# A four-branch decoder trunk: the HGRN forget-gate sigmoids taken from ACT's Sigmoid

## The chip, the core and the metric

The kernel runs on one core of one Trainium2 chip. The metric is device time in microseconds (us), the median of three executions: 3426.57 us, between 3426.15 and 3428.24. Engines are named as in the profile: PE is TensorE (matmuls; PEld is its weight loading), DVE is VectorE, ACT is ScalarE, POOL is GpSimd, SP is SyncE. A name with a q (DVEq, ACTq) is that engine's sequencer. PEclk is the clock granted to TensorE, where 1.00 is 2.4 GHz and 0.50 is 1.2 GHz.

## What is computed

Two layers over 256 tokens at width 2048. In each layer a normalised input h goes through one wide projection, and four token mixers run on slices of it (gated DeltaNet, HGRN2, a diagonal S5, retention), each 1024 wide. They are gated, projected, merged and added to the stream. All is float32. The change touches the HGRN branch only:

```python
def hgrn2_branch(q, f_logit, i_in, g, lb, norm_w):
    q = jax.nn.silu(q)
    log_f = jnp.log(lb + (1.0 - lb) * jax.nn.sigmoid(f_logit))
    k = (1.0 - lb) * jax.nn.sigmoid(-f_logit)
    o = hgrn2_chunked(to_chunks(q), to_chunks(k), to_chunks(i_in), to_chunks(log_f))
    return head_rmsnorm_gate(from_chunks(o), norm_w, g)
```

So both sigmoid(f) and sigmoid(-f) of the forget logit f are needed, for every channel and token.

## The kernel before

**Layout.** Channels lie on the 128 partitions and tokens along the free dimension. A "unit" is 128 channels of every branch (one head each); a layer has 8 units, run as a hardware loop, so there are 16 unit passes. After a layer's units come the GLU of S5, the merge (16 output tiles) and the output projection.

**A unit.** Its frame is the projection: 14 blocks of 128 columns, each in two halves of 8 weight tiles, so 28 calls `project(0)` to `project(27)` on PE. Each call is 24 matmuls, as every product is made from three passes over high and low parts (`w_hi`, `w_lo`, `h_hi`, `h_lo`). Blocks alternate between two PSUM banks, PJ0 and PJ1. The first blocks are HF (the forget logit, halves 0 and 1), GK (2 and 3), GQ (4 and 5), SU (6 and 7) and HQ (8 and 9).

**The weights.** They pass through a ring of four slots. SP's queue loads a half into `raw_w`; ACT copies it to `w_hi` (line 516); DVE subtracts to give `w_lo` (line 896) and so also frees the raw slot. `ahead(i)` on ACT and on DVE makes the copy and the subtraction for the half that `project(i + 4)` uses.

**The order** is written out by hand on each engine. Each engine runs its list strictly in order, and semaphores join the lists. On PE: project(0), project(1), `g_decay_t` (bank GB), project(2), `g_decay_s` (GB), project(3), project(4), `s_turn`, project(5), (6), (7), `g_norms` (GB: sums of squares of the DeltaNet keys and queries, eight matmuls with one moving column), `g_gram_k` (GA), project(8), `s_bu(0)`, `g_gram_q`, project(9), `g_first` (GA), project(10) and so on; from there on a step of the DeltaNet inversion (GA) and a step of HGRN's pairs (`h_pairs`, bank HA) stand between the projections.

On ACT, the start of a unit is: `ahead(0)`, `decays_t` (three exponentials, line 559), the two exponentials of the forget logit (lines 624 and 625), `ahead(1)`, `decays_s` (two exponentials, line 565), two `Sin` for S5 (lines 631, 632), `ahead(2)`, staging of GK (571, 572), `ahead(3)`, a square (637), the copy of `bc_T` (640), `silu_conv(0)` (581, 584), `ahead(4)`, staging of GQ, `ahead(5)`, `silu_conv(1)` (581, 584). The last of these is what `g_norms` waits for. Activation tables are loaded by ACT_TABLE_LOAD instructions that the compiler puts in; they carry the line of the instruction behind them.

On DVE the exponentials become sigmoids: wait for `hsig_staged`, add 1 to both (line 1099), a reciprocal of `hsig[:, 0]` (line 1101), and much later, after `s5_turn(0)` and `ahead(9)`, a reciprocal of `hsig[:, 1]` (line 1148). Then `s5_add(0)` (1033, 1034), and `hf` and `hk` are made from them (1152, 1153). PE's `h_pairs(0)` waits for these. `pj_read`, raised by ACT's second exponential, frees bank PJ0 for `project(4)`.

HGRN's scan is then 8 stages: PE's `h_pairs(s)` gives a bank, DVE's `h_scores(s)` (1058 to 1072) takes it over and rescales the operands for the next stage; its DRAIN on line 1072 frees the bank.

Of the kernel before, what the change touches and what calls it, by code (L numbers as in the profile page):

```python
# [120 lines left out]
def trunk_kernel(nc, A, out):  # L121
    f32, f32r, u8, i32 = mybir.dt.float32, mybir.dt.float32r, mybir.dt.uint8, mybir.dt.int32
    ALU, ACT = mybir.AluOpType, mybir.ActivationFunctionType
    ds = bass.ds
    ctx = ExitStack()
    with ctx:
# [6 lines left out]
        def sem(name):  # L133
            return ctx.enter_context(nc.semaphore(name))
# [67 lines left out]
        def in_work(*shape):  # L202
            n0 = work_at[0]
            work_at[0] += math.prod(shape)
            v = work[:, n0:work_at[0]]
            return v if len(shape) == 1 else v.rearrange("p (a n) -> p a n", a=shape[0])
# [23 lines left out]
        hsig = in_work(2, SEQ)  # L230
# [68 lines left out]
        pj_read = sem("pj_read")  # L299
# [12 lines left out]
        hsig_staged, hsig_used = sem("hsig_staged"), sem("hsig_used")  # L312
# [172 lines left out]
        def _(act):  # L485
            A_ = nc.scalar.activation
# [24 lines left out]
            def split_hi(i, s0, r0):  # L511


                act.wait_ge(split_used, s0 + (i + 1))
                act.wait_ge(raw_full[i % RING], r0 * 16 + 16 * (i // RING + 1))
                A_(w_hi[i % RING][:, :, :], raw_w[i % RING][:, :, :], ACT.Copy).then_inc(hi_ready, 1)  # L516

            with act.Fori(0, DEPTH) as l:
# [21 lines left out]
                with act.Fori(0, UNITS) as u:  # L540
                    n = act.snap(l * UNITS + u)
                    n1 = act.snap(n + 1)
# [4 lines left out]
                    def projected(b):  # L547

                        act.wait_ge(split_used, s0 + (2 * b + 2 + RING))
                        return PJ[b % 2][:, 0:SEQ]  # L550

                    def ahead(i):

                        split_hi(i + RING, s0, r0)

                    def decays_t():
                        act.wait_ge(gb_w, gb0 + 1)
                        for a, c in enumerate((C_NGC0, C_SUF0, C_NGC1)):
                            last = A_(dec_t[:, a, :], GB[:, a * P:(a + 1) * P], ACT.Exp, bias=gcols[:, c:c + 1])
                        last.then_inc(gb_r, 1)  # L560

                    def decays_s():
                        act.wait_ge(gb_w, gb0 + 2)
                        for a, c in enumerate((C_GC0, C_GC1)):
                            last = A_(dec_s[:, a, :], GB[:, a * P:(a + 1) * P], ACT.Exp, bias=gcols[:, c:c + 1])
                        last.then_inc(gb_r, 1)
# [52 lines left out]
                    act.wait_ge(gdn_qkv_used, n1)  # L619
                    decays_t()  # L620

                    act.wait_ge(hsig_used, n1)
                    src = projected(B_HF)
                    A_(hsig[:, 0, :], src, ACT.Exp, scale=-1.0)
                    A_(hsig[:, 1, :], src, ACT.Exp).then_inc(pj_read, 1)
                    act.drain().then_inc(hsig_staged, 1)
                    ahead(1)
                    decays_s()

                    act.wait_ge(phase_ready, l + n1)  # L630
                    A_(s5_sin, s5_p, ACT.Sin, scale=SIN_TURN)
# [151 lines left out]
        def _(dve):  # L783
            TS, TT, STT = nc.vector.tensor_scalar, nc.vector.tensor_tensor, nc.vector.scalar_tensor_tensor
# [108 lines left out]
            def split_lo(i, s0):  # L893

                dve.wait_ge(hi_ready, s0 + (i + 1))
                TT(w_lo[i % RING][:, :, :], raw_w[i % RING][:, :, :], w_hi[i % RING][:, :, :].bitcast(f32),  # L896
                   ALU.subtract).then_inc(raw_used[i % RING], 1)
# [5 lines left out]
            with dve.Fori(0, DEPTH) as l:  # L903
# [77 lines left out]
                with dve.Fori(0, UNITS) as u:  # L981
                    n = dve.snap(l * UNITS + u)
                    n1 = dve.snap(n + 1)
# [18 lines left out]
                    def ahead(i):  # L1002

                        split_lo(i + RING, s0)
# [25 lines left out]
                    def s5_add(half):  # L1030

                        j = slice(2 * half, 2 * half + 2)
                        TT(s5_re[:, j], s5_p[:, 0:2], s5_q[:, 0:2], ALU.add)
                        TT(s5_im[:, j], s5_p[:, 2:4], s5_q[:, 2:4], ALU.subtract)
                        dve.drain()  # L1035
# [59 lines left out]
                    ahead(0)  # L1095
                    ahead(1)

                    dve.wait_ge(hsig_staged, n1)
                    TS(hsig[:, :, :], hsig[:, :, :], 1.0, None, ALU.add)
                    dve.drain()  # L1100
                    nc.vector.reciprocal(hsig[:, 0, :], hsig[:, 0, :])
                    ahead(2)
                    conv_taps(0)
                    ahead(3)
# [40 lines left out]
                    dve.wait_ge(sincos_ready, n1)  # L1145
                    s5_turn(0)
                    ahead(9)
                    nc.vector.reciprocal(hsig[:, 1, :], hsig[:, 1, :])
                    s5_add(0)
                    dve.wait_ge(hgrn_used, n1)  # L1150
                    lb0, lb1 = (lb[:, ds(u, 1), c:c + 1].rearrange("p a b -> p (a b)") for c in range(2))
                    TS(hf[:, :], hsig[:, 0, :], lb1, lb0, ALU.mult, ALU.add)
# [134 lines left out]
                with dve.Fori(0, MT) as t:  # L1287
# [3 lines left out]
                    for pair in range(2):  # L1291
                        for i in range(6 * pair, 6 * pair + 4):
                            split_lo(i + RING, s0)
                        for m in (2 * pair, 2 * pair + 1):
# [5 lines left out]
                            src = (SA, SB)[m % 2][:, 0:SEQ]  # L1300
# [492 lines left out]
```

## Time and profile before

| What | Value |
|---|---|
| Three executions | 3426.15, 3426.57, 3428.24 us |
| Profiled execution, first to last instruction (span) | 3423.5 us; the profile gives no other time of it |
| PE busy | 3199.7 us (93%), 25656 matmuls |
| DVE busy | 2193.0 us (64%) |
| ACT busy | 1446.7 us (42%) |
| POOL busy | 286.3 us (8%) |
| Mean granted TensorE clock | 0.975 |
| One unit pass | about 117 us, 16 of them |

The page of the profile has the busy time of each engine, the span in 40 slices, the DMA queues, the chain of work that ended last, and the costliest groups of instructions. The trace can also be asked for the waits, the chain in order of time, the timeline of one engine, and the busy time and clock of a chosen stretch. PE's matmuls overlap in the timeline: each 128x256 one is shown as 0.28 us, but they start 0.12 us apart at the full clock.

### The profile page before, as it was taken

What the parts mean: (1) busy time and instruction counts of PE and PEld (TensorE: products, weight loads), DVE (VectorE), ACT (ScalarE), POOL (GpSimd) and SP (SyncE); (2) the same over time, 40 slices, a digit from 0 to 9 for tenths busy, and PEclk for the clock granted to TensorE, in tenths of its full rate; (3) what the DMA queues carried; (4) which work ended last, traced back from release to release, by engine and by line L of the source; (5) the groups of instructions that cost most, each with busy time, mean ns of one, the idle gap of its engine ahead of it and who ended that gap; (6) DMA issues with size and microseconds to landing.
All of it is one profiled execution on the core that took longest, in us unless ns stands there. A gap on an engine that the chain in (4) does not pass through costs nothing.

```text
span 3423.5 us, 69661 instructions
## 1 busy us (share of the span) xinstructions
PE 3199.7 (93%) x25656; PEld 3115.1 (91%) x25656; DVE 2193.0 (64%) x3451; ACT 1446.7 (42%) x2083; POOL 286.3 (8%) x530
## 2 busy tenths in 40 slices
PE   5999999999989999999989999999999899999997
PEld 4998989898888999999988988899898799999997
DVE  5777877787784555555457877877787555555553
ACT  2454345444443433444344444344434443343341
POOL 2011101101100000000011011101110100000000
PEclk7999999999999999999979999999999999999998
DMA  3454445444544666666634444444444466666662
GB/s 100 123 136 126 132 121 140 120 132 127 140 130 138 181 183 182 181 183 167 174 90 122 129 133 133 127 121 135 128 130 123 117 185 183 182 181 182 184 166 86
DMA packets 942788, 492.15 MB, mean 144 GB/s; under 512 B 18448, under 2 KB 938608, under 8 KB 942032
## 3 DMA queue, kind: packets, MB, share of 16 engines
q1 hardware_dynamic: 932704, 471.46, 50.1%
q0 software_dynamic: 9152, 13.11, 1.5%
q10 hardware_dynamic: 688, 4.33, 0.3%
q8 instruction: 153, 2.51, 0.3%
q14 instruction: 91, 0.75, 0.1%
HBM read 486.73 MB, written 2.10 MB: 143 GB/s over the span
## 4 chain that ended last, share of the span: by engine, by line
PE 35%; issue 32%; DVE 15%; DVEq 11%; ACT 5%; ACTq 2%; DMA 1%; POOL 0%; POOLq 0%
PE PJ L1350 23%; PE S L1350 6%; DVEq L1017 3%; DVE w_lo L896 2%; DVEq L1067 2%; PE GA L1350 2%; PE GB L1350 1%; DVE work L1015 1%; PE RA L1350 1%; DVEq L1072 1%; DVE region L1042 1%; ACT w_hi L516 1%; DVEq L1035 1%; DVE region L1050 1%; DMA region<-s_glu_w 1%
## 5 line engine op out<-in xcount | busy, mean ns | idle before, releaser
L1350 PE MATMUL PJ<-h_hi,w_hi 128*128 128x256 f32 x6144 | 1780.0, 290 | 51.9 <-issue 41.9
L1350 PE MATMUL PJ<-h_hi,w_lo 128*128 128x256 f32 x6144 | 1746.4, 284 | 0.0
L1350 PE MATMUL PJ<-h_lo,w_hi 128*128 128x256 f32 x6144 | 1746.4, 284 | 0.0
L896 DVE TENSOR_TENSOR w_lo<-raw_w,w_hi 128x1024 fp32r<-128x1024 f32 x896 | 1092.7, 1223 | 648.6 <-ACT w_hi L516 606.1
L516 ACT ACTIVATE w_hi<-raw_w 128x1024 fp32r<-128x1024 f32 x896 | 946.6, 1057 | 871.1 <-PE PJ L1350 616.6
L1350 PEld LDWEIGHTS PJ<-h_hi,w_hi 128*128 128x128 f32 x6144 | 1187.2, 193 | 67.7 <-issue 67.7
L1350 PEld LDWEIGHTS PJ<-h_lo,w_hi 128*128 128x128 f32 x6144 | 1187.7, 193 | 0.0
L1350 PEld LDWEIGHTS PJ<-h_hi,w_lo 128*128 128x128 f32 x6144 | 1185.9, 193 | 0.0
L1350 PE MATMUL S<-y_parts_a,w_hi 128*128 128x256 f32 x1280 | 309.5, 283 | 0.0
L1350 PEld LDWEIGHTS S<-y_parts_a,w_hi 128*128 128x128 f32 x1280 | 227.3, 192 | 0.0
L1350 PE MATMUL GA<-work 128*128 128x128 f32 x1280 | 189.5, 278 | 10.9 <-DVEq L1017 10.2
L1350 PEld LDWEIGHTS GA<-work 128*128 128x128 f32 x1280 | 164.8, 191 | 19.7 <-DVEq L1017 14.3
L600 ACT ACTIVATE work<-GA 128x256 f32<-128x256 f32 x96 | 36.9, 384 | 286.0 <-PE GA L1350 286.0
L1350 PE MATMUL S<-y_parts_b,w_hi 128*128 128x256 f32 x512 | 144.9, 283 | 0.0
L1350 PE MATMUL S<-y_parts_b,w_lo 128*128 128x256 f32 x512 | 144.9, 283 | 0.0
L1350 PE MATMUL HA<-hq,hk 128*128 128x128 f32 x544 | 94.0, 293 | 37.8 <-DVEq L1072 36.8
L1050 DVE TENSOR_TENSOR region<-region 128x1024 f32<-128x1024 f32 x96 | 117.6, 1225 | 13.8 <-issue 10.9
L1350 PEld LDWEIGHTS HA<-hq,hk 128*128 128x128 f32 x544 | 71.8, 190 | 56.0 <-DVEq L1072 52.1
L455 POOL TENSOR_TENSOR h_ms<-h_ms,eps_p 128x2 f32<-128x2 f32 x16 | 18.6, 1163 | 989.7 <-ACTq L692 989.7
L1350 PEld LDWEIGHTS S<-y_parts_b,w_hi 128*128 128x128 f32 x512 | 98.3, 192 | 0.0
L1350 PEld LDWEIGHTS S<-y_parts_b,w_lo 128*128 128x128 f32 x512 | 98.3, 192 | 0.0
L1350 PE MATMUL PJ<-y_all,region 128*128 128x256 f32 x256 | 61.6, 399 | 26.6 <-DMA region<-s_glu_w 26.4
(325 smaller groups left out, 2918.3 us busy)
## 6 DMA issues: line engine op xcount, KB each, us to landing
raw_w<-w_in SPq DMA_DIRECT2D x704, 512.0 KB, 3.7
raw_w<-w_branch SPq DMA_DIRECT2D x128, 512.0 KB, 4.0
raw_w<-w_out SPq DMA_DIRECT2D x64, 512.0 KB, 4.2
region<-s_glu_w POOLq DMA_DIRECT2D x16, 512.0 KB, 4.4
region<-x ACTq DMA_DIRECT2D x1, 2048.0 KB, 11.8
ret_decay<-c_ret POOLq DMA_DIRECT2D x16, 128.0 KB, 3.2
out<-region ACTq DMA_DIRECT2D x1, 2048.0 KB, 6.4
b_raw<-s_b_re POOLq DMA_DIRECT2D x64, 8.0 KB, 2.6
```

Source lines behind the costliest of these rows:

```text
L455: nc.gpsimd.tensor_tensor(ms[:, 2:4], ms[:, 0:2], eps_p[:, :], ALU.add)
L516: A_(w_hi[i % RING][:, :, :], raw_w[i % RING][:, :, :], ACT.Copy).then_inc(hi_ready, 1)
L600: A_(rr[:, :, :], GA[:, 0:2 * P], ACT.Copy).then_inc(ga_r, 1)
L896: TT(w_lo[i % RING][:, :, :], raw_w[i % RING][:, :, :], w_hi[i % RING][:, :, :].bitcast(f32), ALU.subtract).then_inc(raw_used[i % RING], 1)
L1015: TT(tt[:, first:4, :].rearrange("p a n -> p (a n)"), tt[:, first:4, :].rearrange("p a n -> p (a n)"), GA[:, first * P:4 * P], ALU.subtract)
L1017: dve.drain().then_inc(ga_r, 1)
L1035: dve.drain()
L1042: nc.vector.tensor_tensor_scan(v[:, j, :], mag, v[:, j, :], 0.0, ALU.mult, ALU.add)
L1050: TT(a, b, c, op)
L1067: dve.drain()
L1072: dve.drain().then_inc(ha_r, 1)
L1350: return nc.tensor.matmul(o, w, m, start=start, stop=stop)
```

## The change

ACT now makes the two sigmoids directly, with its Sigmoid function (once with scale -1). They move behind `ahead(1)` and `decays_s`, so that they stand directly ahead of the two Sin. DVE loses the addition, its drain and both reciprocals; its wait for `hsig_staged` moves from the start of the unit to just before `hf` is made.

```diff
@@ ACT
                     decays_t()
 
+                    ahead(1)
+                    decays_s()
+
                     act.wait_ge(hsig_used, n1)
                     src = projected(B_HF)
-                    A_(hsig[:, 0, :], src, ACT.Exp, scale=-1.0)
-                    A_(hsig[:, 1, :], src, ACT.Exp).then_inc(pj_read, 1)
+                    A_(hsig[:, 0, :], src, ACT.Sigmoid)
+                    A_(hsig[:, 1, :], src, ACT.Sigmoid, scale=-1.0).then_inc(pj_read, 1)
                     act.drain().then_inc(hsig_staged, 1)
-                    ahead(1)
-                    decays_s()
 
                     act.wait_ge(phase_ready, l + n1)
@@ DVE
                     ahead(1)
 
-                    dve.wait_ge(hsig_staged, n1)
-                    TS(hsig[:, :, :], hsig[:, :, :], 1.0, None, ALU.add)
-                    dve.drain()
-                    nc.vector.reciprocal(hsig[:, 0, :], hsig[:, 0, :])
                     ahead(2)
@@ DVE
                     s5_turn(0)
                     ahead(9)
-                    nc.vector.reciprocal(hsig[:, 1, :], hsig[:, 1, :])
                     s5_add(0)
+                    dve.wait_ge(hsig_staged, n1)
                     dve.wait_ge(hgrn_used, n1)
```

## Rows read from the trace of the kernel before

**Rows 1.** The page, part 1: busy us (share of span) and instructions.

```profile
PE 3199.7 (93%) x25656; PEld 3115.1 (91%) x25656; DVE 2193.0 (64%) x3451; ACT 1446.7 (42%) x2083; POOL 286.3 (8%) x530
```

**Rows 2.** Waits of the whole span: who waited for whom, us, times, longest.

```profile
PE PJ L1350 <- issue: 41.9, 14, 3.2
...
PE HA L1350 <- DVEq L1072: 36.8, 80, 0.7
...
PE RA L1350 <- DVEq L1191: 13.2, 16, 0.8
```

**Rows 3.** The chain that ended last, 318 to 346 us: start, us, what.

```profile
326.57 1.28 ACT L631
327.86 1.01 ACT region L631
...
340.76 0.43 ACT region L584
...
341.30 1.05 PE GB L1350 x8
```

**Rows 4.** The same chain, 340 to 440 us.

```profile
355.77 1.66 DVEq L1035
```

**Rows 5.** Timeline of ACT, start of the third unit: start, us, what [idle before].

```profile
322.92 0.39 ACT L624 ACTIVATE work<-PJ 128x256 f32<-128x256 f32 x1
323.18 0.40 ACT L625 ACTIVATE work<-PJ 128x256 f32<-128x256 f32 x1
323.75 1.06 ACT L516 ACTIVATE w_hi<-raw_w 128x1024 fp32r<-128x1024 f32 x1 [0.17 <-issue]
325.92 0.63 ACT L565 ACTIVATE work<-GB,gcols 128x128 f32<-128x128 f32 x2 [1.11 <-PE GB L1350]
326.57 1.28 ACT L631 ACT_TABLE_LOAD   x1
```

**Rows 6.** Groups of ACT's instructions over the whole span.

```profile
L763 ACT ACTIVATE conv_in<-PJ 128x256 f32<-128x256 f32 x128 | 47.0, 367 | 0.0
...
L631 ACT ACT_TABLE_LOAD x16 | 20.5, 1283 | 0.3
...
L744 ACT ACT_TABLE_LOAD x8 | 10.3, 1283 | 39.4 <-PE PJ L1350 39.4
```

**Rows 7.** Timeline of DVE, the same unit.

```profile
330.85 1.23 DVE L896 TENSOR_TENSOR w_lo<-raw_w,w_hi 128x1024 fp32r<-128x1024 f32 x1 [2.60 <-ACT w_hi L516]
...
351.26 0.42 DVE L1141 SCALAR_TENSOR_TENSOR work<-GA,sq 128x256 f32<-128x256 f32 x1 [0.68 <-PE GA L1350]
...
355.69 1.75 DVE L1148 RECIPROCAL work<-work 128x256 f32<-128x256 f32 x1
357.35 0.63 DVE L1033 TENSOR_TENSOR region<-region 128x512 f32<-128x512 f32 x1
```

**Rows 8.** Timeline of PE, the same unit.

```profile
328.60 0.28 PE L1350 MATMUL PJ<-h_hi,w_hi 128*128 128x256 f32 x1
...
341.30 1.05 PE L1350 MATMUL GB<-ones,region 128*128 128x1 f32 x8 [0.59 <-ACT region L584]
...
401.40 0.48 PE L1350 MATMUL RA<-rx 128*128 128x256 f32 x1 [0.83 <-DVEq L1191]
```

**Rows 9.** Windows: stretch, length, PE PEld DVE ACT POOL busy (x), PEclk, DMA share, GB/s.

```profile
197.00:203.00 6.00, 5.87 (x48) 5.66 (x48) 1.22 (x4) 2.34 (x2) 2.54 (x8) 1.00 0.37 101
315.00:318.30 3.30, 3.30 (x18) 3.30 (x17) 0.42 (x2) 0.28 (x1) 1.93 (x6) 0.50 0.60 166
...
2571.30:2574.50 3.20, 3.20 (x16) 3.20 (x16) 1.18 (x3) 0.00 (x0) 0.75 (x3) 0.50 0.35 85
...
1714.40:1728.00 13.60, 12.87 (x61) 12.78 (x61) 7.07 (x9) 3.32 (x5) 0.45 (x1) 0.50 0.58 155
```

**Rows 10.** Timeline of PE: start of layer two, and the last loop turn.

```profile
1713.88 13.38 PE L1350 MATMUL GA<-ones,region 128*128 128x1 f32 x64 [2.60 <-ACT region L508]
...
2571.05 0.52 PE L1350 MATMUL PJ<-h_hi,w_hi 128*128 128x256 f32 x1 [2.71 <-issue]
```

## The prediction

> **What bounds the kernel now.** I read the busy shares first. PE is busy for 93% of the span, DVE for 64%, ACT for 42% [rows 1]. This says that the end is set by how long PE waits, and not who makes it wait. The list of waits tells that for the units: PE waits on DVE's drain of line 1072, the end of each HGRN score stage, 80 times and 36.8 us in all, and on the drain of line 1191 for 13.2 us, and it pauses for 41.9 us at 14 loop turns, 2.99 us each, for nothing that the profile shows [rows 2]. The two DVE waits make 50.0/16 = 3.1 us a unit.
>
> The chain in order of time splits a unit into stretches with different owners. I read it for the third unit; the others are alike.
> - Start of the unit: the chain runs along ACT. From the end of `decays_s` ACT is packed: table load, two Sin, copies, stagings, SiLUs, up to the square at 340.76, and PE's `g_norms` follows it at 341.30 [rows 3]. PE stands idle for 0.59 us before it [rows 8]. So **ACT is late there by 0.59 us already**; whatever it gains in work after `decays_s` PE waits for in full.
> - Then PE runs without a wait, and DVE waits for PE (0.68 us before line 1141) [rows 7].
> - From there to 401.40 the chain runs along DVE. The second reciprocal lies in it: the 1.66 us for which the sequencer stands at line 1035 are the time that the reciprocal runs [rows 4].
> - The last quarter is PE's own.
>
> Early in a unit ACT is the bound and in its middle DVE is, though neither is busy all the time. The change takes from the one and gives to the other.
>
> **The change part by part.**
>
> *DVE, line 1148.* One instruction of 1.75 us, but the next starts 1.66 us after it [rows 7], and that is what leaves the chain. PE's waits on DVE behind this point, 3.1 us a unit [rows 2], are more than 1.66, so it can pass on whole: **-1.66 us a unit**. The moved wait adds a semaphore instruction; its data are ready some 30 us before, so it costs a step of the sequencer: 0, at most 0.1 us.
>
> *DVE, lines 1099 and 1101.* The reciprocal has the shape of the other, 1.75 us, and behind it DVE stands idle for 2.60 us, for ACT's copy [rows 7]. The time goes into that idle: 0. With ACT later still, the cover grows.
>
> *ACT, before `decays_s`.* The two exponentials and their drain take 322.92 to 323.75 less some overlap; then ACT copies a weight half and waits 1.11 us for PE's `g_decay_s` [rows 5]. Taking them out only lengthens this wait: 0. `ahead(1)` comes 0.8 us sooner, and project(5) needs it much later: 0.
>
> *ACT, behind `decays_s`.* Here each nanosecond counts. The two sigmoids have the shape of the exponentials: from 322.92 to 323.58, 0.66 us for the pair. The Sigmoid of the merge takes 367 ns from PSUM, against 392 and 402 for these [rows 5, 6], so the function is not dearer; I keep 0.66. The drain and the semaphore step add 0.17 us, the gap before line 516 [rows 5]. And there is a table load: 1.28 us [rows 5, 6]. A load stands where Exp turns into Sin (line 631), Sin into SiLU (581), and before the GLU's Sigmoid, behind GELU (744) [rows 6]. Exp and Sigmoid never follow each other directly, nor do Sigmoid and Sin, so whether such a pair shares a table is not shown; at the kernel's start a Tanh (line 501) follows an Exp without a load, so sharing exists. Bounds: 0, if Sigmoid shares a table with one of its two neighbours, and 1.28. I take 1.28, since it has to share with the one or the other of just these two. The sum is 0.66 + 0.17 + 1.28 = **+2.11 us a unit**, all of it ahead of `g_norms`.
>
> The Trainium skill, "ScalarE: Activation LUTs", section "Table sets: the hidden batching unit", lists exp and sigmoid as anchors of different sets, which no row here could show. Its section "What ACT_TABLE_LOAD costs" puts a switch at 2.66 us, load and drain; here the Sin starts 1.29 us after the load starts [rows 3], with no drain behind. By the page the sum would be 1.38 x 16 = 22 us higher.
>
> *Who stands behind the later ACT.* project(4) needs the forget logit read out of PJ0. That is now at 323.58; it will be at 326.57 + 1.28 + 0.66 = 328.51. PE starts project(4) at 328.60 [rows 8]: a tie, 0 to 0.1 us, and it falls into PE's later wait. DVE's subtractions for project(6) and (7) come 2.1 us later; that for project(6) ended at 332.08 and is wanted at about 334.7 (328.60, two projections of 24 x 0.122 us and `s_turn`), so it still fits. SP's loads and POOL's queue follow engines that are not late there: 0. Then PE stands before `g_norms` for 0.59 + 2.11 = 2.70 us.
>
> *TensorE's clock.* This pause is about as long as the pauses at the loop turns, 2.99 us on average [rows 2]. Behind 9 of these 14 the granted clock fell to 0.50, behind 5 it stayed at 1.00 (one that stayed, the first and the last that fell: [rows 9]); the pause ahead of the last fall was 2.71 us [rows 10]. Behind the new pause come eight one-column matmuls, 1.05 us. Such matmuls did not bring the clock up: PE ran 64 of them for 13.38 us at 0.50 [rows 9, 10]. So pause and these together are 3.75 us of nearly nothing, and I expect a fall in 14 units of 16. Price: at half clock PE did 16 matmuls in 3.20 us; at full clock 48 take 5.87, 0.122 each [rows 9]. 3.20 - 16 x 0.122 = 1.25 us, up to 1.4 with the ends, say 1.3; PE bounds the stretch behind, so it passes on. 14 x 1.3 = **+18 us**. Bounds: 0 and 16 x 1.4 = 22.
>
> **The sum.** 16 x 2.11 = 33.8; 18; 16 x -1.66 = -26.6. Together +25.2 us. The span is 3423.5, the median of the runs 3426.6, 3.1 above it; I add the change to the median: **3452 us**.
>
> **The rivals.**
> 1. *The clock does not fall, or seldom.* For it: 5 of 14 such pauses passed. Against it: the one-column matmuls. Then 16 x (2.11 - 1.66) = +7, 3434 us; with half of the falls 3443. The Trainium skill, "TensorE: Matmul & The Clock Gate", rules for kernel authors, warns only of gaps of more than about 3 us, by which 2.70 would pass; the trace has a fall behind 2.71, so rule and row differ.
> 2. *Faster: no table load is added.* Place: between `decays_s` and Sin. ACT is then late by 0.66 + 0.17 = 0.83 only, less than DVE's 1.66. PE's pause is 1.42 us, shorter than any behind which the clock fell in a unit. 16 x (0.83 - 1.66) = -13.3: 3413 us. It decides from the point where ACT's delay, with what the clock costs, is under 1.66. If the one-column matmuls count as pause and half of the units fall, it is 3424, no change. For it: the unseen pair; against it: Sigmoid behind GELU, Sin behind Exp and SiLU behind Sin each needed a load.
> 3. *DVE's gain is lost.* If behind line 1148 DVE soon waits for a late PE, as 0.68 us at line 1141 hints [rows 7], some or all of the 1.66 us is not passed on: up to 26.6 more, 3479 us. Against it: PE catches up 3.1 us there [rows 2].
> 4. *The load is dearer*, 1.38 us more for a drain: 3474 us. The rows of three loads a unit speak against it [rows 3, 5].
>
> That the change does something else than it says is hardly possible: two reciprocals a unit leave DVE for sure.
>
> **How the numbers follow.** Forecast (load, falls in most units) 0.62; rival 1 0.16; rival 2 0.10, half of it as no change; rival 3 0.08; rival 4 0.03; 0.01 left. A measurement of this kernel can tell about 0.2% from no change, 6.9 us: slower means above 3433.4, faster below 3419.7. Faster: half of rival 2 and a little, 0.06. No change: the other half and the low edge of rival 1, 0.09. Slower: 0.85. The forecast's own range, with 10 to 16 falls of 1.25 to 1.4 us, is 3444 to 3458. For 8 in 10 I reach down over rival 1 to 3432 and up into rival 3 to 3465.
>
> **What would show it.** Right: a fourth table load in each unit, x16 more, 1283 ns each, ahead of line 626 or so; Sin later by 2.1 us against line 565; PE idle before `g_norms` 2.7 us, releaser line 584; windows at 0.50 behind it; no RECIPROCAL of 1.75 us in the units; PE's waits on lines 1072 and 1191, now 50.0 us, down to about 50.0 - 26.6 = 23. Wrong: no fourth load, a pause of 1.4 us; a clock of 1.00 behind it; waits on line 1072 unchanged, or DVE waiting for PE in the score stages.

## The result and the profile after

The changed kernel takes 3466.85 us (3465.75 to 3469.89, four runs) against 3426.75 us for the one before: a ratio of 1.0117, 95% interval 1.0103 to 1.0132, **slower by 40 us**. 3452 us were forecast, between 3432 and 3465. The direction and the mechanism were right; the size lies 2 us over the upper end.

The profiled execution has a span of 3464.8 us, 41.2 more (unrounded) than the 3423.5 of before. Busy times, page, part 1, which answer to [rows 1]:

```profile
PE 3225.6 (93%) x25656; PEld 3147.7 (91%) x25656; DVE 2136.0 (62%) x3403; ACT 1467.4 (42%) x2099; POOL 285.6 (8%) x530
```

DVE has lost 57 us of work and ACT has gained 21, yet PE, whose matmuls are the same 25656, is busy for 26 us more: they run at a lower clock. The groups of ACT show where the new table load stands, ahead of line 627, the first Sigmoid:

```profile
L516 ACT ACT_TABLE_LOAD x16 | 20.5, 1283 | 101.0 <-PE PJ L1347 101.0
L627 ACT ACT_TABLE_LOAD x16 | 20.5, 1283 | 0.3
L632 ACT ACT_TABLE_LOAD x16 | 20.5, 1283 | 2.7 <-issue 2.7
L581 ACT ACT_TABLE_LOAD x16 | 20.5, 1283 | 0.3
```

ACT's timeline in the third unit, which answers to [rows 5]:

```profile
331.40 0.63 ACT L565 ACTIVATE work<-GB,gcols 128x128 f32<-128x128 f32 x2 [1.94 <-PE GB L1347]
332.05 1.28 ACT L627 ACT_TABLE_LOAD   x1
333.34 0.38 ACT L627 ACTIVATE work<-PJ 128x256 f32<-128x256 f32 x1
333.62 0.38 ACT L628 ACTIVATE work<-PJ 128x256 f32<-128x256 f32 x1
334.17 1.28 ACT L632 ACT_TABLE_LOAD   x1 [0.17 <-issue]
335.46 1.06 ACT L632 ACTIVATE region<-region 128x1024 f32<-128x1024 f32 x1
```

From line 565 to the first Sin there are 4.06 us, before 1.94 [rows 3, 5]: 2.12 us more. What had been taken away in front of line 565 has become idle time (1.94 us where 1.11 stood). PE and DVE in the same unit, DVE's row on `hf` (line 1149) with its counterpart in the kernel before (line 1152) behind it:

```profile
348.89 1.15 PE L1347 MATMUL GB<-ones,region 128*128 128x1 f32 x8 [2.56 <-ACT region L584]
...
409.00 0.69 PE L1347 MATMUL RA<-rx 128*128 128x256 f32 x2 [0.82 <-DVEq L1188]
```

```profile
360.42 0.42 DVE L1138 SCALAR_TENSOR_TENSOR work<-GA,sq 128x256 f32<-128x256 f32 x1 [0.68 <-PE GA L1347]
...
363.70 1.23 DVE L897 TENSOR_TENSOR w_lo<-raw_w,w_hi 128x1024 fp32r<-128x1024 f32 x1 [0.17 <-issue]
364.84 0.68 DVE L1034 TENSOR_TENSOR region<-region 128x512 f32<-128x512 f32 x1
...
366.46 0.42 DVE L1149 TENSOR_SCALAR hf<-work,lb 128x256 f32<-128x256 f32 x1 [0.34 <-issue]
```

```profile
358.84 0.41 DVE L1152 TENSOR_SCALAR hf<-work,lb 128x256 f32<-128x256 f32 x1 [0.27 <-issue]
```

Three marks split a unit, counted from its line 565: `g_norms` (the GB row), the first DVE step that waits for `g_first` (line 1138, line 1141 before), and the RA row, where PE's last wait on DVE in the unit ends. The rest, from there to the next unit's line 565, is called the turn. This table is worked out from such rows of every unit, and so are all "stretches" below:

| us | before | after | difference |
|---|---|---|---|
| line 565 to `g_norms` | 15.38 | 17.50 | +2.12 |
| `g_norms` to line 1141 / 1138 | 9.96 | 11.50 | +1.54 |
| line 1141 / 1138 to RA<-rx | 50.11 | 48.60 | -1.52 |
| line 565 to RA<-rx, mean of 16 | 75.46 | 77.59 | +2.13 |
| RA<-rx to the next line 565, mean of 14 ("turn") | 41.67 | 41.94 | +0.27 |

16 x 2.13 = 34.1, the 14 turns together 587.2 - 583.3 = 3.9, and 3.2 us are left outside the units: 41.2. The windows of the kernel after show the clock. Columns as in [rows 9]:

```profile
346.40:349.00 2.60, 0.11 (x1) 0.11 (x2) 2.23 (x4) 1.40 (x4) 0.00 (x0) 1.00 0.61 172
350.00:353.00 3.00, 3.00 (x15) 3.00 (x15) 1.62 (x7) 1.99 (x3) 1.63 (x2) 0.50 0.85 220
```

PE stands still, and behind that the granted clock is 0.50, in 16 units of 16; before it was 1.00 there in all. Such a drop from 1.00 to 0.50 is called a fall below, and a double one where the half-clock stretch is twice as long. Waits of the whole span, which answer to [rows 2]:

```profile
PE GB L1347 <- ACT region L584: 41.1, 16, 2.6
...
PE PJ L1347 <- issue: 40.7, 14, 3.0
...
PE HA L1347 <- DVEq L1073: 23.2, 48, 0.6
PE RA L1347 <- DVEq L1188: 13.2, 16, 0.8
```

The HGRN waits have gone from 36.8 to 23.2 us and from 80 to 48 times: in each unit two of five score stages no longer hold PE up. These 13.6 us are less than the 16 x 1.52 = 24.3 that the table gives, since idle time before an instruction is only part of its delay here (PE's ends are modelled). In the third unit it is 0.06, 0, 0.18 and 0.67 us before `h_pairs(0)` to `h_pairs(3)`; without the reciprocal and at the same clock (e1 below) these four start 0.23, 0.31, 0.66 and 1.53 us sooner behind `g_norms`, and the later ones by no more.

### The profile page after: what moved, and what is told of

Its sections match the earlier page's. It is cut to its first block, busy times and chain, and to the rows that moved or that the text cites. A ratio compares the mean times of both kernels' runs of the same rounds, so it can differ in the third digit from the quotient of the medians.

```text
span 3464.8 us, 69645 instructions
## 1 busy us (share of the span) xinstructions
PE 3225.6 (93%) x25656; PEld 3147.7 (91%) x25656; DVE 2136.0 (62%) x3403; ACT 1467.4 (42%) x2099; POOL 285.6 (8%) x530
## 4 chain that ended last, share of the span: by engine, by line
PE 35%; issue 32%; DVE 14%; DVEq 10%; ACT 5%; ACTq 2%; DMA 1%; POOL 0%; POOLq 0%
PE PJ L1347 24%; PE S L1347 6%; DVE w_lo L897 2%; DVEq L1018 2%; DVEq L1068 2%; PE GA L1347 2%; ACT w_hi L516 1%; PE GB L1347 1%; DVE work L1016 1%; DVEq L1073 1%; PE RA L1347 1%; DVE region L1043 1%; DVE region L1051 1%; DMA region<-s_glu_w 1%; ACTq L636 1%
## 5 line engine op out<-in xcount | busy, mean ns | idle before, releaser
L1347 PE MATMUL PJ<-h_hi,w_hi 128*128 128x256 f32 x6144 | 1794.2, 292 | 50.7 <-issue 40.7
L1347 PEld LDWEIGHTS PJ<-h_hi,w_hi 128*128 128x128 f32 x6144 | 1200.5, 195 | 68.0 <-issue 66.5
L1347 PEld LDWEIGHTS PJ<-h_lo,w_hi 128*128 128x128 f32 x6144 | 1199.9, 195 | 0.0
L1347 PEld LDWEIGHTS PJ<-h_hi,w_lo 128*128 128x128 f32 x6144 | 1198.4, 195 | 0.0
L1347 PE MATMUL HA<-hq,hk 128*128 128x128 f32 x544 | 90.8, 287 | 24.3 <-DVEq L1073 23.2
```

What stands on the lines that cost most here:

```text
L1347: return nc.tensor.matmul(o, w, m, start=start, stop=stop)
```

## The experiments

The ratios are to the kernel before, run on the same chip, where its median was 3429 to 3432 us; its 37 executions there took 3425.6 to 3435.4 us. The changed kernel itself was not run again. e1, e2 and e3 leave the HGRN branch without its right sigmoids; the others compute the whole. Each diff says against which kernel it is, with "..." where lines are left out. **Theory A** is that of the prediction: ACT's lateness before `g_norms` passes on in full, the clock falls behind PE's pause, DVE's reciprocal passes on as a gain. Its rivals were B (the slow stretch behind `g_norms` has another cause than the clock) and C (DVE's part is worth nothing).

### e1: DVE's half alone

Against the kernel before; the wait for `hsig_staged` stands before `hf`, as in the change.

```diff
-                    A_(hsig[:, 0, :], src, ACT.Exp, scale=-1.0)
-                    A_(hsig[:, 1, :], src, ACT.Exp).then_inc(pj_read, 1)
+                    A_(hsig[:, 0, :], src, ACT.Tanh, scale=0.5)
+                    A_(hsig[:, 1, :], src, ACT.Tanh, scale=-0.5).then_inc(pj_read, 1)
...
-                    dve.wait_ge(hsig_staged, n1)
-                    TS(hsig[:, :, :], hsig[:, :, :], 1.0, None, ALU.add)
-                    dve.drain()
-                    nc.vector.reciprocal(hsig[:, 0, :], hsig[:, 0, :])
...
-                    nc.vector.reciprocal(hsig[:, 1, :], hsig[:, 1, :])
...
+                    dve.wait_ge(hsig_staged, n1)
```

> The kernel before with only DVE's part of the change: no addition, no reciprocals, wait moved. The two exponentials on ACT are replaced in place by two Tanh of the same shape (Tanh follows Exp without a table load in the trace), so that the values stay bounded; the HGRN branch is not computed rightly. Theory A (DVE's reciprocal of line 1148 lies on the path and its removal is worth 1.5 us a unit): 3427 - 16 x 1.53 = 3402 us, between 3398 and 3406, PE's waits on the HGRN drain down by about 20 us, PE's pause before g_norms unchanged at 0.59 us, no half clock behind it. Rival C (DVE's gain is never passed on, DVE then waits for PE): within 5 us of the kernel before, 3422 to 3427.

3408.09 us, ratio 0.9934 (0.9918 to 0.9951), 2 us over the expected range. Waits of e1:

```profile
PE HA L1346 <- DVEq L1072: 23.2, 48, 0.6
...
PE GB L1346 <- ACT region L584: 9.5, 16, 0.6
```

The stretch to RA<-rx is 73.94 us, 1.52 less than before: that is the full worth of the reciprocal, and C falls. The listed HGRN waits are down by 13.6 us and not by about 20. The 1.52 us make 24.3; 21 came between the medians. Between the two profiled executions the turns gave 5.7 us back (42.08 us on average, 41.67 before), though nothing was changed in them, and the time outside the units 6.4; but e1's profiled execution is the slowest of its four, by 4 us, so these two are not what the medians lost.

### e2: ACT's half alone

Against the changed kernel.

```diff
+                    dve.wait_ge(hsig_staged, n1)
+                    TS(hsig[:, :, :], hsig[:, :, :], 1.0, None, ALU.add)
+                    dve.drain()
+                    nc.vector.reciprocal(hsig[:, 0, :], hsig[:, 0, :])
                     ahead(2)
...
+                    nc.vector.reciprocal(hsig[:, 1, :], hsig[:, 1, :])
                     s5_add(0)
-                    dve.wait_ge(hsig_staged, n1)
```

> The changed kernel with DVE's addition and both reciprocals put back where they were (applied to the sigmoids, so the HGRN branch is not computed rightly). Theory A: 3467 + 24.5 = 3491 us, 3487 to 3496; pause before g_norms 2.57 us and half clock behind it in all units. Rival C (DVE's part is worth nothing): 3467 us within 5.

3498.42 us, ratio 1.0195 (1.0178 to 1.0212). The two halves add up to the change: +2.0% and -0.7% against +1.2%. Six of the 16 units had a half-clock stretch of double length behind `g_norms`, which cost 3.1 us instead of 1.5 (13.06 us to DVE's next mark against 11.50). That is 9 us, more than the 2 us over the expected upper end.

### e3: the same late place without the table load

Against the changed kernel.

```diff
-                    A_(hsig[:, 0, :], src, ACT.Sigmoid)
-                    A_(hsig[:, 1, :], src, ACT.Sigmoid, scale=-1.0).then_inc(pj_read, 1)
+                    A_(hsig[:, 0, :], src, ACT.Tanh, scale=0.5)
+                    A_(hsig[:, 1, :], src, ACT.Tanh, scale=-0.5).then_inc(pj_read, 1)
```

> The changed kernel with Tanh (scale 0.5 and -0.5) in place of the two Sigmoids, at the same late place, so that no fourth table load is needed (HGRN not computed rightly). Theory A: ACT is late by 0.83 instead of 2.12 us, PE's pause before g_norms 1.3 to 1.45 us; if the clock does not fall behind it, 3427 + 16 x (0.83 - 1.53) = 3416 us; if it falls in all units, 3440 us; I expect falls in some units, so 3416 to 3432. A rival in which the load itself is not what costs (Sigmoid is slow, or the reordering of ahead(1) and decays_s): 3455 us or more.

3427.47 us, ratio 0.9997 (0.9988 to 1.0007): **without the load the change is no change**, in the expected range. `g_norms` comes 16.07 us behind line 565, so ACT is late by 0.69 us and not by 0.83. The changed kernel has 17.50 there: the load of 1.28 us cost 1.42. Its rows tell the rest: without a load the first of the two functions starts 0.52 us after line 565, overlapping it (327.67 against 327.15), while the load starts only when line 565 has ended, 0.65 us after its start (332.05 against 331.40). ACT's rows of e3:

```profile
327.15 0.62 ACT L565 ACTIVATE work<-GB,gcols 128x128 f32<-128x128 f32 x2 [1.94 <-PE GB L1347]
327.67 0.38 ACT L627 ACTIVATE work<-PJ 128x256 f32<-128x256 f32 x1
```

PE's pause is 1.29 us, and the clock fell behind it in 5 units of 16. So one kernel shows both cases. Windows behind `g_norms` in the third unit and in the fourth, and DVE's step that ends the stretch:

```profile
346.00:349.00 3.00, 3.00 (x25) 2.50 (x24) 2.16 (x9) 1.45 (x2) 1.13 (x2) 1.00 0.94 267
462.50:465.50 3.00, 3.00 (x17) 3.00 (x16) 1.98 (x9) 0.66 (x1) 1.31 (x2) 0.54 0.99 286
```

```profile
353.19 0.42 DVE L1138 SCALAR_TENSOR_TENSOR work<-GA,sq 128x256 f32<-128x256 f32 x1 [0.68 <-PE GA L1347]
...
471.36 0.42 DVE L1138 SCALAR_TENSOR_TENSOR work<-GA,sq 128x256 f32<-128x256 f32 x1 [0.67 <-PE GA L1347]
```

Line 565 of these units begins at 327.15 and 443.83, so the distances are 26.04 and 27.53 us. The difference, 1.49 us, is what one fall costs here.

### e4: PE's pause filled with work

Against the changed kernel.

```diff
                     project(7)
+                    for k in range(20):
+                        MM(SB[:, 0:SEQ], h_hi[:, k % KT, 0:P], h_hi[:, (k + 1) % KT, :])
                     g_norms()
```

> The changed kernel, output and all, with 20 extra projection-shaped matmuls (0.12 us each, 2.4 us) in front of PE's wait of g_norms, into a PSUM bank that is free, so that PE works through its pause. Nothing else is changed, ACT is as late as before. Theory A (the clock falls because PE pauses, and this costs 1.56 us a unit): no half clock behind g_norms, first decay of the stretch to line 1141 back from 11.5 to 10.0 us, 3467 - 25 = 3442 us, 3438 to 3446. Rival B (the stretch behind g_norms is slow for another reason: weights, banks or POOL late): 3467 us or a little more, since work was added.

3447.89 us, ratio 1.0054 (1.0038 to 1.0071): the kernel does 320 useless matmuls more and is 0.6% faster than the changed kernel by the two ratios. Its timeline and a window behind it:

```profile
341.69 2.56 PE L1347 MATMUL S<-h_hi 128*128 128x256 f32 x20
344.43 1.05 PE L1347 MATMUL GB<-ones,region 128*128 128x1 f32 x8 [0.18 <-ACT region L584]
```

```profile
345.50:348.50 3.00, 3.00 (x27) 3.00 (x28) 1.65 (x6) 2.02 (x3) 1.63 (x2) 1.00 0.87 218
```

`g_norms` comes no sooner (17.50 us behind line 565), but the clock stays at 1.00 and the stretch behind it is 9.96 us again in all 16 units. So the 1.54 us were the clock, and B falls. The time is 2 us over the expected range; in the profiled execution the turns take 42.37 us on average, six of them with a double half-clock stretch.

### e5: Tanh in place of both sigmoids

Against the kernel before. DVE's wait, addition and reciprocals are gone as in e1, and `lb` has a third column.

```diff
-                    A_(hsig[:, 0, :], src, ACT.Exp, scale=-1.0)
-                    A_(hsig[:, 1, :], src, ACT.Exp).then_inc(pj_read, 1)
+                    A_(hsig[:, 0, :], src, ACT.Tanh, scale=0.5).then_inc(pj_read, 1)
...
-                TS(lb[:, :, 1], lb[:, :, 0], -1.0, 1.0, ALU.mult, ALU.add)
+                TS(lb[:, :, 1], lb[:, :, 0], -0.5, 0.5, ALU.mult, ALU.add)
+                TS(lb[:, :, 2], lb[:, :, 0], 0.5, -0.5, ALU.mult, ALU.add)
+                TS(lb[:, :, 0], lb[:, :, 0], 0.5, 0.5, ALU.mult, ALU.add)
...
-                    TS(hk[:, :], hsig[:, 1, :], lb1, None, ALU.mult)
+                    TS(hk[:, :], hsig[:, 0, :], lb2, lb1, ALU.mult, ALU.add)
```

> The whole computation, built on the kernel before: one Tanh(f/2) in place of the two exponentials, where they stood (Tanh shares Exp's table by the trace); sigmoid(f) and sigmoid(-f) are (1 + t)/2 and (1 - t)/2, and these constants go into the per-channel columns with which DVE makes hf and hk anyway. No addition, no reciprocals, no further table load. Theory A: as e1, stretch from line 565 to RA<-rx 73.9 us (75.5 before), pause before g_norms 0.59 us, 3408 us on a chip where the kernel before takes 3429, or 3402 to 3407 where it takes 3427: faster by 0.5 to 0.75%. A rival, that e1 owed its gain to values near zero or one and not to the missing work: 3427.

3409.43 us, ratio 0.9935 (0.9922 to 0.9949), with three table loads a unit as before and a stretch to RA<-rx of 74.00 us: as expected. The gain of e1 was the missing work and not its wrong values.

### e6: Sigmoid in ACT's idle time

Against the kernel before. The two exponentials and their drain are gone from where the copy stands, and DVE's part is as in e1.

```diff
                     src = projected(B_HF)
+                    A_(hsig[:, 0, :], src, ACT.Copy).then_inc(pj_read, 1)
...
                     ahead(8)
+                    A_(hsig[:, 1, :], hsig[:, 0, :], ACT.Sigmoid, scale=-1.0)
+                    A_(hsig[:, 0, :], hsig[:, 0, :], ACT.Sigmoid)
+                    act.drain().then_inc(hsig_staged, 1)
```

> The whole computation with the Sigmoid function: the forget logit is only copied out of its bank where the exponentials stood, and the two Sigmoids run from this copy behind ahead(8), where ACT stands idle for 3.66 us a unit in the kernel before (it waits for PE). They bring two table loads, 2.57 us, 0.7 us of work and a drain, together 3.5 us. Theory A (place, not the function or the number of loads, sets the price): pause before g_norms 0.59 us, stretch to RA<-rx 73.9 to 74.1 us, same time as e5 within 4 us, with five table loads a unit. Rival (each added load costs its 1.28 us wherever it stands): 3408 + 16 x 2.57 = 3449 us.

3413.4 us, ratio 0.9945 (0.993 to 0.9961), with **five** table loads a unit. ACT's timeline:

```profile
344.21 1.06 ACT L516 ACTIVATE w_hi<-raw_w 128x1024 fp32r<-128x1024 f32 x1 [1.54 <-PE PJ L1347]
345.28 1.28 ACT L652 ACT_TABLE_LOAD   x1
346.58 0.42 ACT L652 ACTIVATE work<-work 128x256 f32<-128x256 f32 x1
346.90 0.40 ACT L653 ACTIVATE work<-work 128x256 f32<-128x256 f32 x1
347.46 1.28 ACT L657 ACT_TABLE_LOAD   x1 [0.16 <-issue]
348.92 0.39 ACT L657 ACTIVATE hq<-PJ 128x256 f32<-128x256 f32 x1 [0.18 <-PE PJ L1347]
```

Before line 657 there are 0.18 us of waiting for PE left of 3.66: the slot is full, and nothing is late. The stretch to RA<-rx is 73.96 us, as in e1. The time is 4.0 us above e5's, at the edge of what was expected, and the two intervals overlap.

### e7: the exponentials moved late, nothing else

Against the kernel before.

```diff
+                    ahead(1)
+                    decays_s()
                     A_(hsig[:, 0, :], src, ACT.Exp, scale=-1.0)
                     A_(hsig[:, 1, :], src, ACT.Exp).then_inc(pj_read, 1)
                     act.drain().then_inc(hsig_staged, 1)
-                    ahead(1)
-                    decays_s()
```

> The kernel before with its two exponentials moved behind ahead(1) and decays_s, as the change places the sigmoids; all else, DVE's reciprocals too, as before. Theory A: ACT late by 0.69 us, pause 1.29 us, DVE's part 0, the clock falls behind the pause in 4 to 7 units at 1.5 us each: 3429 + 11 + 8 = 3448 us, 3442 to 3454. Rival (the move costs nothing by itself, PE has slack): 3429.

3461.83 us, ratio 1.0088 (1.0072 to 1.0103), above the expected range. The move alone costs almost 1%. Within the units all is as expected: 0.69 us later, 7 falls, a mean stretch to RA<-rx of 76.82 us (+1.36, 22 us). The turns are where more came: 42.50 us, seven of 14 with a double half-clock stretch, +0.83 each, 12 us. Together that is 34 us against the profiled execution of the kernel before; against its median on this chip, 3431.66 us, the move costs 30.

### e8: Sigmoid early

Against the changed kernel.

```diff
                     decays_t()
-                    ahead(1)
-                    decays_s()
-
...
                     A_(hsig[:, 0, :], src, ACT.Sigmoid)
                     A_(hsig[:, 1, :], src, ACT.Sigmoid, scale=-1.0).then_inc(pj_read, 1)
                     act.drain().then_inc(hsig_staged, 1)
+                    ahead(1)
+                    decays_s()
```

> The changed kernel with the two Sigmoids back where the exponentials stood, ahead of ahead(1) and decays_s. It needs five table loads a unit, one more than the changed kernel, since Exp comes back. Theory A: the load and the work in front of decays_s mostly fill ACT's wait for PE there; ACT is late by 1.3 to 1.5 us instead of 2.12, pause about 2.0 us, falls behind it in 10 to 16 units: 3436 to 3455 us, so faster than the changed kernel by 12 to 30 us though it loads more. Rival (loads add up): 3467 + 20 = 3487 us.

3457.46 us, ratio 1.0073 (1.0057 to 1.0088). One load more than the changed kernel, and the ratio is lower, as expected; but 2 us above the range. PE's pause is 2.22 us and not 2.0, ACT being late by 1.63 us; the clock fell behind it in 14 units. The profiled execution is the slowest of the four (3464.36 us).

### e9: the pause filled in part

Against the changed kernel.

```diff
+                    for k in range(6):
+                        MM(SB[:, 0:SEQ], h_hi[:, k % KT, 0:P], h_hi[:, (k + 1) % KT, :])
                     g_norms()
```

> The changed kernel with only 6 extra matmuls (0.73 us) in front of PE's wait of g_norms, where e4 had 20. The pause left is about 1.85 us, between e3's 1.29 us (the clock fell in 5 of 16 units) and the change's 2.57 us (16 of 16). Theory A (a fall hangs on how long PE pauses and on the moment at which the pause comes): falls in 7 to 14 units, 1.5 us each; in each unit the stretch to line 1141 is either 10.0 or 11.5 us behind g_norms and nothing between; 3447 to 3467 us. Rival (the price grows smoothly with the pause): all units alike, between 10.0 and 11.5.

3467.72 us, ratio 1.0108 (1.0091 to 1.0125), 0.7 us over the range. A miss in the count: with a pause of 1.85 us the clock fell in all 16 units, twice for double the length. The stretch behind `g_norms` is 11.4 to 11.5 us in the 14 and 13.1 in the two, nothing between, so the price does come in steps. Filling 0.73 of the 2.57 us gave back nothing that can be told from the change (1.0117).

### e10: work added near the loop turn

Against the changed kernel.

```diff
                     g_turn()
+                    for k in range(6):
+                        MM(SB[:, 0:SEQ], h_hi[:, k % KT, 0:P], h_hi[:, (k + 1) % KT, :])
                     project(27)
```

> The changed kernel with 6 extra matmuls (0.73 us) in front of project(27), near the end of each unit, where PE has no pause. It tells whether the falls behind the loop turns (14 of 14 in the changed kernel, 9 of 14 before) hang on the moment at which the turn comes. Theory A: the pattern changes: turns with no fall (41.2 us from RA<-rx to the next line 565, and 0.7 added) or with a double one (43.2) appear beside single ones (42.0); mean time 3467 + 12 us, plus or minus 8 for the turns; falls behind g_norms stay at 14 to 16 of 16. Rival (each turn falls because PE's pause before g_norms has made it so): still 14 single falls of 14, 3479 us.

3469.04 us, ratio 1.0114 (1.0097 to 1.0131). Neither came whole: 14 of 14 turns still have one half-clock stretch, as the rival said, but the time is below what both gave, for of the 0.73 us added to each unit only 0.16 show (turn 42.10 us). Waits:

```profile
PE PJ L1347 <- issue: 33.0, 14, 2.9
```

PE's pause at the turn went from 40.7/14 = 2.91 to 2.36 us and took 0.55 of the 0.73. What ends this pause, the profile does not show.

### e11 and e12: one more step off ACT's list before `g_norms`

```diff
                     ahead(3)
-                    A_(s5_cos, s5_cos, ACT.Square, scale=math.sqrt(2.0))
...
                     ahead(6)
+                    A_(s5_cos, s5_cos, ACT.Square, scale=math.sqrt(2.0))
+                    act.drain()
                     A_(s5_cos, s5_cos, ACT.Copy, scale=-1.0, bias=1.0).then_inc(sincos_ready, 1)
```

e11 is this on e5, e12 is this on the changed kernel.

> e5 with one more step: the square of s5_cos (line 637, 0.95 us on ACT) moved from in front of silu_conv(0) to behind ahead(6), so that it no longer stands in front of g_norms. The whole computation. Theory A (PE waits before g_norms for ACT's packed list, 0.59 us a unit even in e5): the pause goes to 0.1 us or less, 16 x 0.5 to 0.6 = 8 to 9 us less than e5, and the remaining 0.4 us of the moved work gives nothing: 3400 us where the kernel before takes 3431, a ratio of 0.991, the loop turns plus or minus 4 us. Rival (DVE or PE bound there): e5's time.

> The changed kernel with the same move of the square. ACT is 0.95 us less late: pause before g_norms 1.6 us instead of 2.57, all of the 0.95 passed on, 15 us. Falls of the clock behind it in 10 to 16 of 16 units (e9 fell in all with 1.85 us, e3 in 5 with 1.29): 3467 - 15 - (0 to 9) = 3443 to 3452 us, on a chip where the kernel before takes 3431 up to 3456. Rival (the price of a pause is the fall alone, ACT's lateness itself does not count): 3467.

e11: **3395.34 us, ratio 0.9894 (0.9878 to 0.9911)**, the fastest kernel of the study, with the whole computation. Its `g_norms`, and that of e12:

```profile
336.17 0.95 PE L1348 MATMUL GB<-ones,region 128*128 128x1 f32 x8
```

```profile
343.96 1.05 PE L1348 MATMUL GB<-ones,region 128*128 128x1 f32 x8 [1.62 <-ACT region L584]
```

In e11 PE no longer waits there, and the stretch to RA<-rx is 73.18 us, 0.82 less than in e5, somewhat more than the 0.5 to 0.6 expected. e12: 3443.52 us, ratio 1.0038 (1.0024 to 1.0052), in its range; the pause is 0.95 us shorter, and the clock fell in 9 units (10 to 16 were expected).

## Why the prediction was right and wrong

**Right, each by its row.** The fourth load is there, 1283 ns, with no drain behind it. ACT is late by 2.12 us, forecast 2.11, and all of it reaches `g_norms`. That this is so near is in part luck: the two functions with their drain cost 0.69 us and not 0.83, and the load 1.42 and not 1.28 (e3). The first reciprocal and the addition gave nothing: the stretches to `g_norms` and on to DVE's mark are the same in e1 as before. project(4) started 2.73 us behind line 565, 2.68 before. DVE's gain passes on: 1.52 us a unit, forecast 1.66. DVE's own rows show 1.53, from line 1141 to `hf` 7.58 us before and 6.05 after; the moved wait, priced at 0 to 0.1, has taken some of the rest (idle before `hf` 0.27, now 0.34). One sign failed: PE's waits on lines 1072 and 1191 were to go from 50.0 down to about 23 us and are at 36.4, since that list has only part of the gain. The clock falls behind the pause, because of the pause (e4). Rivals 1 to 4 are out: 16 falls of 16; a load; C refuted by e1; no drain.

**Wrong: the clock term**, "14 x 1.3 = +18 us. Bounds: 0 and 16 x 1.4 = 22". It was 16 x 1.54 = 24.6 us, outside its own bounds. The count was too low by two, and the price was read from a window of 3.20 us laid inside a half-clock stretch, with matmuls counted that had begun before it. The right reading is the one of e3, the same stretch of work at both clocks: 1.49 us, and 1.48 to 1.58 in the units of the changed kernel.

**Wrong: a term was missing.** The turns were taken as they were, with 9 falls behind 14. After the change all 14 have one, +3.9 us; before, a turn with a fall took 41.91 us and one without 41.24, so the five more account for 3.4 of it. A longer pause before `g_norms` is not needed for them: e1, e5 and e6 have none beyond the old 0.59 us, yet 11, 13 and 13 of their turns have falls and take 42.08, 41.99 and 42.07 us. The profiled execution of the kernel before, at 41.67, has the cheapest turns of all measured here (the others lie between 41.94 and 42.50; e8, whose line 565 itself comes later, is left out). That is partly that one execution: its mean clock is 0.975, while the 37 executions of the same kernel beside the experiments have 0.975 at 3425.6 us and 0.971 at 3435.4, though nothing in it differs. So the falls differ from execution to execution of one kernel as well, and how much of the 3.9 us is owed to the change is not shown. Outside the units 3.2 us came. A part of it is the half clock at the first GLU. Its matmuls began at 1021.87 us before and at 1041.43 after; before, the clock was at 1.00 from 1025 on, after, it was still at 0.50 when they had run for 4.6 us. Windows of the kernel before, and of the one after:

```profile
1025.00:1028.00 3.00, 3.00 (x16) 2.64 (x15) 0.00 (x0) 0.74 (x1) 0.21 (x1) 1.00 0.02 6
```

```profile
1036.00:1046.00 10.00, 4.57 (x11) 3.67 (x12) 5.54 (x5) 5.63 (x6) 1.88 (x2) 0.50 0.57 159
```

The sum again, with the measured terms: ACT +33.9, clock behind `g_norms` +24.6, DVE -24.3, turns +3.9, outside +3.2: 41.3, against 41.2 of span. The forecast had 33.8, 18, -26.6, 0, 0. So the miss of 16 us is 7 from the size of the clock term, 2 from DVE's, 7 from the terms left out. One slip of the prediction is in its own range as well: 10 falls of 1.25 us and 16 of 1.4 add up to 3446 and 3456, not to 3444 and 3458.

What stays open: why a fall comes once, twice or not at all, at a turn (11 of 14 in e2, 14 of 14 in e7 with seven double) and before `g_norms` at pauses of 1.29 to 2.57 us, and what ends PE's pause at a turn. e10 was to tell of the turns and did not.

## What to carry to other kernels

Ask of an engine not how busy it is but in which stretch others wait for it: here a table load of 1.28 us cost 1.42 us (and a clock fall) behind `decays_s`, and two of them cost nothing behind `ahead(8)` (e6). When TensorE's pause in a dense kernel grows, here from 0.59 us (no fall) to 1.29 us and more (falls in 5 units of 16 and up), price it twice, as the pause and as the matmuls behind it at half clock, from a stretch that the trace shows at both levels. Before a difference of a few us is put down to a change, compare it with what executions of one kernel differ by, here 10 us. And where a sigmoid is wanted beside exponentials, (1 + tanh(x/2))/2 runs from the table that is already loaded.

## What the runs showed of the hardware beyond what was expected

- Falls of the granted clock by the length of PE's pause in front of eight one-column matmuls, out of 16 units: 0 and 0.18 us (e11, e4) none; 0.59 (before) none; 1.29 (e3, e7) 5 and 7; 1.62 (e12) 9; 1.85 (e9) 16; 2.22 (e8) 14; 2.57 (after, e2, e10) 16. So falls come behind pauses well under those of the turns (2.71 to 3.2 us, 9 of 14 before). That the thin matmuls behind the pause have a part in it is likely and not shown: no run has the pause without them. The Trainium skill, "TensorE: Matmul & The Clock Gate", section "Why this matters for your kernels", warns of gaps over about 3 us; here 1.29 us was enough in some units.
- Behind `g_norms` a fall costs a step, 1.49 us in e3 and 1.48 to 1.58 in the changed kernel, or 3.1 us when it is double (e2, e9), never something between. At a turn, where PE pauses anyway, it costs 0.67 us (before).
- Tanh runs from Exp's table without a load (e5, 16 units), Sigmoid does not, nor does Sin run from Sigmoid's (after). A load of 1283 ns put between two functions costs 1.42 us, for the overlap of the two is lost as well (e3 against after).
- 0.73 us of matmuls placed before the last projection of a unit cost 0.16 us: PE's pause at the loop turn shrank by 0.55 (e10).
